# Sums of squares with tokens on partitions in the scan mixer of a two-block kernel

## The reference, cut to what matters

```python
kk = heads(k * k_k)                                   # [b, n, 12, 64]
kk = kk / jnp.maximum(jnp.sqrt(jnp.sum(kk * kk, axis=-1, keepdims=True)), 1e-12)
...
mu = jnp.mean(y, axis=-1, keepdims=True)              # y: sum of both directions' scans
var = jnp.mean(jnp.square(y - mu), axis=-1, keepdims=True)
yn = ((y - mu) * lax.rsqrt(var + GN_EPS)).reshape(b, n, D_RWKV) * gn_w + gn_b
```

## Time and profile before

| | us |
|---|---|
| runs, median of 3 (lowest to highest) | 3272.98 (3271.57 to 3274.49) |
| profiled execution, first to last instruction (span) | 3270.0 |
| TensorE matmuls busy | 3175.3 |
| VectorE busy | 2170.2 |
| ScalarE busy | 541.8 |
| GpSimd busy | 171.0 |

### The profile page before, as it was taken

One profiled execution on the slowest core, in us unless ns is written; L12 is line 12 of the kernel. 1 busy time (PEld: TensorE's weight loads), 2 busy tenths in 40 slices (PEclk: granted clock), 3 DMA queues, 4 the chain that ended last, 5 costly groups with the idle time before them and its releaser, 6 DMA issues.

```text
span 3270.0 us, 64614 instructions
## 1 busy us (share of the span) xinstructions
PE 3175.3 (97%) x28090; PEld 2861.1 (87%) x28090; DVE 2170.2 (66%) x4656; ACT 541.8 (17%) x1073; POOL 171.0 (5%) x200
## 2 busy tenths in 40 slices
PE   7999999899999999999999999999999999999998
PEld 3888445588888999999889999999999999999998
DVE  6887337566676476675657667776676576776774
ACT  2000010234433110110111011121110102120111
POOL 1000000122222010000000000000000000000000
PEclk9999999999999999999999999999999999999999
DMA  7456656100000245455245564334444443334443
GB/s 290 172 217 223 235 205 231 44 7 6 7 7 7 80 168 180 155 168 181 96 165 168 172 222 158 118 121 143 154 170 174 144 166 105 129 123 168 142 168 117
DMA packets 69229, 466.46 MB, mean 143 GB/s; under 512 B 7296, under 2 KB 9984, under 8 KB 16217
## 3 DMA queue, kind: packets, MB, share of 16 engines
q1 hardware_dynamic: 51696, 368.07, 32.2%
q0 software_dynamic: 12192, 87.04, 7.2%
q10 hardware_dynamic: 5065, 7.27, 0.7%
HBM read 456.59 MB, written 5.77 MB: 141 GB/s over the span
## 4 chain that ended last, share of the span: by engine, by line
PE 91%; DVE 6%; ACT 2%; DMA 1%; issue 1%; POOL 0%; ACTq 0%; DVEq 0%; POOLq 0%
PE ps L785 32%; PE ps L1279 18%; PE ps L840 8%; PE ps L680 7%; PE ps L1430 4%; PE ps L864 4%; PE ps L902 1%; PE ps L915 1%; PE ps L921 1%; PE ps L1298 1%; PE ps L1176 1%; PE ps L1353 1%; PE ps L1224 1%; PE ps L1328 1%; DMA arena<-in_ada_t 1%; PE ps L962 1%
## 5 line engine op out<-in xcount | busy, mean ns | idle before, releaser
L785 PE MATMUL ps<-arena 128*128 128x128 f32 x4400 | 519.1, 275 | 0.0
L785 PEld LDWEIGHTS ps<-arena 128*128 128x128 f32 x4400 | 505.0, 192 | 0.0
L785 PE MATMUL ps<-arena,ring 128*128 128x128 f32 x2200 | 275.0, 275 | 0.0
L1875 DVE TENSOR_TENSOR arena<-arena,ps 128x256 f32<-128x256 f32 x146 | 61.5, 421 | 309.4 <-ACT arena L1481 283.5
L785 PEld LDWEIGHTS ps<-arena,ring 128*128 128x128 f32 x2200 | 260.9, 192 | 0.5
L2005 DVE CUSTOM_DVE_ANT_0 arena<-arena,vec 128x1024 f32<-128x1024 f32 x168 | 206.7, 1281 | 1.7 <-DMA arena<-in_ada_t 1.6
L1279 PE MATMUL ps<-y,arena 128*128 128x128 f32 x1584 | 193.3, 276 | 0.6 <-DVE y L2502 0.6
L1279 PEld LDWEIGHTS ps<-y,arena 128*128 128x128 f32 x1584 | 184.6, 192 | 4.8 <-issue 3.4
L1840 DVE TENSOR_TENSOR arena<-ring 128x512 f32<-128x512 f32 (+1 forms) x170 | 113.9, 670 | 61.2 <-DMA ring<-in_w_f_down 33.3
L680 PE MATMUL ps<-arena,ring 128*128 128x512 f32 x352 | 152.2, 592 | 0.0
L680 PEld LDWEIGHTS ps<-arena,ring 128*128 128x128 f32 x352 | 66.9, 190 | 83.8 <-issue 83.7
(11 more groups left out here) (395 smaller groups left out, 5847.6 us busy)
## 6 DMA issues: line engine op xcount, KB each, us to landing
ring<-in_w_f_gu SPq DMA_DIRECT2D x88, 1024.0 KB, 4.9
arena<-in_ada_t POOLq DMA_DIRECT2D x72, 1024.0 KB, 5.3
ring<-in_w_fx_gu SPq DMA_DIRECT2D x44, 1024.0 KB, 4.8
ring<-in_w_f_down SPq DMA_DIRECT2D x36, 1024.0 KB, 4.8
ring<-in_w_fx_down SPq DMA_DIRECT2D x24, 1024.0 KB, 4.8
ring<-in_w_qk_a SPq DMA_DIRECT2D x18, 1024.0 KB, 4.8
ring<-in_w_qk_r SPq DMA_DIRECT2D x16, 1024.0 KB, 4.8
ring<-in_w_v_r SPq DMA_DIRECT2D x16, 1024.0 KB, 4.8
```

The costliest lines, as they stand in the source:

```text
L785: last = mm(out, weights[number][:, j * P:(j + 1) * P], inputs[number](base + j), start=(s.opens and j == 0 and number in (1, 5)), stop=(s ...
```

## The change

The squares become the stationary operand of a product whose moving operand is two columns of `blk`, the first column of each head. The result has tokens on partitions: for the keys four chunks of 128 tokens by two heads, 8 columns (`key_rows`), for the readout two chunks, 4 columns (`y_rows`). Clamp, root and reciprocal work on these. To bring the scales back to channels on partitions, one product for each chunk and head has the column, repeated 64 times, as stationary operand and the identity as moving operand (`key_back`, 8 products; `readout_back`, 4 products); VectorE then multiplies from PSUM (`key_unit` for the keys, in one piece of 512 columns). `key_back` is at step 5 of an even unit, behind `chunk_u`; `readout_back` at step 8. The readout's last four VectorE operations move to step 9. `key_products` waits for one more step. For t = 0, `key_back` is behind all slots of e_in, `key_inverse` ahead of slot 9 on VectorE, `key_unit` behind slot 10, and TensorE starts the mixer after it.

```diff
+        def head_columns():
+            return blk[:, 0:P:64]
+        def back_bank(u):
+            return 3 if unit(u) else 6
+        def over_head(rows, c, hd):
+            return rows[:, c, hd:hd + 1].to_broadcast([P, 64])
...
-                mm(ps[:, norm_sums(t), :], blk[:], kk, start=True, stop=True).then_inc(*step(f"pe.kk_sum{t}"))
+                for c in range(4):
+                    last = mm(ps[:, norm_sums(t), 2 * c:2 * c + 2], kk[:, c * P:(c + 1) * P], head_columns(), start=True, stop=True)
+                last.then_inc(*step(f"pe.kk_sum{t}"))
+
+            def key_back(t):
+                pe.wait_ge(*past(f"dve.kk_rows{t}"))
+                for c in range(4):
+                    for hd, rows in enumerate((FIRST, SECOND)):
+                        last = mm(ps[rows, norm_sums(t), c * P:(c + 1) * P], over_head(key_rows, c, hd), ident[:],
+                                  start=True, stop=True)
+                last.then_inc(*step(f"pe.kk_back{t}"))
...
+            key_back(0)
...
-            pe.wait_ge(*past("dve.kk_max0"))
+            pe.wait_ge(*past("dve.kk0"))
...
+                        pe.wait_ge(*past(f"dve.gn_n{t}"))
...
-                mm(ps[:, 5, 0:SEQ], blk[:], gn_sq, start=True, stop=True).then_inc(*step(f"pe.gn_var{t}"))
+                for c in range(LAT):
+                    last = mm(ps[:, 5, 2 * c:2 * c + 2], gn_sq[:, c * P:(c + 1) * P], head_columns(), start=True, stop=True)
+                last.then_inc(*step(f"pe.gn_var{t}"))
+
+            def readout_back(t, u):
+                pe.wait_ge(*past(f"dve.gn_rows{t}"))
+                if unit(u):
+                    pe.wait_ge(*past(f"act.k_tok{u}"))
+                for c in range(LAT):
+                    for hd, rows in enumerate((FIRST, SECOND)):
+                        last = mm(ps[rows, back_bank(u), c * P:(c + 1) * P], over_head(y_rows, c, hd), ident[:], start=True, stop=True)
+                last.then_inc(*step(f"pe.gn_back{t}"))
...
+                    elif n == 5 and u:
+                        key_back(u // 2)
...
+                if t is not None and n == 8:
+                    readout_back(t, u)
...
-                f(kk, kk, ACT.Sqrt).then_inc(*step(f"act.kk_std{t}"))
+                rows = key_rows.rearrange("p c h -> p (c h)")
+                f(rows, rows, ACT.Sqrt).then_inc(*step(f"act.kk_std{t}"))
...
-                ts(kk, ps[:, norm_sums(t), :], 1e-24, None, ALU.max).then_inc(*step(f"dve.kk_max{t}"))
-
-            def key_inverse(t, n):
+                ts(key_rows.rearrange("p c h -> p (c h)"), ps[:, norm_sums(t), 0:8], 1e-24, None, ALU.max) \
+                    .then_inc(*step(f"dve.kk_max{t}"))
+
+            def key_inverse(t):
                 v.wait_ge(*past(f"act.kk_std{t}"))
-                half = slice(SEQ * (n // 2 - 2), SEQ * (n // 2 - 1))
-                nc.vector.reciprocal(kk[:, half], kk[:, half]).then_inc(*step(f"dve.kk_inv{t}_{n}"))
-                v.wait_ge(*past(f"dve.kk_inv{t}_{n}"))
-                tt(kk[:, half], kk[:, half], kkr[:, half], ALU.mult).then_inc(*step(f"dve.kk{t}_{n}"))
+                rows = key_rows.rearrange("p c h -> p (c h)")
+                nc.vector.reciprocal(rows, rows).then_inc(*step(f"dve.kk_rows{t}"))
+
+            def key_unit(t):
+                v.wait_ge(*past(f"pe.kk_back{t}"))
+                tt(kk, ps[:, norm_sums(t), :], kkr, ALU.mult).then_inc(*step(f"dve.kk{t}"))
...
-                elif s.l == 9:
-                    key_inverse(0, 4)
-                    key_inverse(0, 6)
+                elif s.l == 10:
+                    key_unit(0)
...
-                    elif n in (4, 6) and u:
-                        key_inverse(u // 2, n)
+                    elif n == 4 and u:
+                        key_inverse(u // 2)
+                    elif n == 6 and u:
+                        key_unit(u // 2)
...
-                        nc.vector.reciprocal(gn_std, gn_std).then_inc(*step(f"dve.gn_rstd{t}"))
-                        v.wait_ge(*past(f"dve.gn_rstd{t}"))
-                        tt(gn_cen, gn_cen, gn_std, ALU.mult).then_inc(*step(f"dve.gn_n{t}"))
-                    elif n == 8:
+                        rows = y_rows.rearrange("p c h -> p (c h)")
+                        nc.vector.reciprocal(rows, rows).then_inc(*step(f"dve.gn_rows{t}"))
+                    elif n == 9:
+                        v.wait_ge(*past(f"pe.gn_back{t}"))
+                        tt(gn_cen, gn_cen, ps[:, back_bank(u), 0:SEQ], ALU.mult).then_inc(*step(f"dve.gn_n{t}"))
```

More of the change, by code:

```diff
@@ L382, in program @@
         mid, carry = take(2, 4), take(3, 4)
+        key_rows, y_rows = take(4, 2), take(2, 2)
         tri = y[:, 1, 0:4, :].rearrange("p (q x) t -> p q (x t)", q=2) \
@@ L1608, in fill @@
                         act.wait_ge(*past(f"pe.gn_var{t}"))
-                        f(gn_std, ps[:, 5, 0:SEQ], ACT.Sqrt, bias=V("gneps"), scale=1.0 / 64) \
+                        f(y_rows.rearrange("p c h -> p (c h)"), ps[:, 5, 0:2 * LAT], ACT.Sqrt, bias=V("gneps"), scale=1.0 / 64) \
                             .then_inc(*step(f"act.gn_std{t}"))
@@ L2130, in key_clamp @@
                 v.wait_ge(*past(f"pe.kk_sum{t}"))
-                ts(kk, ps[:, norm_sums(t), :], 1e-24, None, ALU.max).then_inc(*step(f"dve.kk_max{t}"))
-            def key_inverse(t, n):
+                ts(key_rows.rearrange("p c h -> p (c h)"), ps[:, norm_sums(t), 0:8], 1e-24, None, ALU.max) \
+                    .then_inc(*step(f"dve.kk_max{t}"))
+            def key_inverse(t):
                 v.wait_ge(*past(f"act.kk_std{t}"))
-                half = slice(SEQ * (n // 2 - 2), SEQ * (n // 2 - 1))
-                nc.vector.reciprocal(kk[:, half], kk[:, half]).then_inc(*step(f"dve.kk_inv{t}_{n}"))
-                v.wait_ge(*past(f"dve.kk_inv{t}_{n}"))
-                tt(kk[:, half], kk[:, half], kkr[:, half], ALU.mult).then_inc(*step(f"dve.kk{t}_{n}"))
+                rows = key_rows.rearrange("p c h -> p (c h)")
[3 more added lines that the diff above has]
+                tt(kk, ps[:, norm_sums(t), :], kkr, ALU.mult).then_inc(*step(f"dve.kk{t}"))
             for s in slots_flat("e_in"):
+                if s.l == 9:
+                    key_inverse(0)
                 v.wait_ge(slots_used, s.n + 1)
@@ L2315, in fill @@
                     elif n == 7:
-                        v.wait_ge(*past(f"dve.kk{u // 2}_6"))
+                        v.wait_ge(*past(f"dve.kk{u // 2}"))
                         key_scales(u)
```

## The result

The changed kernel takes 3285.54 us, the median of five runs (3284.59 to 3286.08), against 3272.93 (3271.51 to 3274.49) for the kernel before on the same chip: ratio 1.004, 95% interval 1.0029 to 1.0051, or 12.6 us more. 3286.0 was predicted.

The account below looks back on a forecast made before the run. The prediction took TensorE's in-order matmuls to bound the kernel. Its terms, 4.3 + 2.5 + 1.0 + 1.8 + 0.75 + 2.8 = 13.1 us, on 3273.0 gave 3286 us, range 3277 to 3294.

Parts of the forecast that it names:

- the start: Hand-over from e_in to the mixer: features waits for the last slot's whole handling and the unit key, +4.3 us.
- the readouts: Ordinary readouts: readout_back costs TensorE 0.75 us, up to 0.3 of it hidden; net +0.45, four times, +1.8 us.
- p = 12: Readout at p = 12: TensorE is never idle there, so readout_back's full 0.75 us counts.
- the end: Last readout: readout_back stands behind ten e_out products, with VectorE's four operations only after it, +2.8 us.
- the even units: Even units, t = 1 to 5: key_back fills the hole at level_x 4; +0.2 us a unit, +1.0 in all.
- the clock: After TensorE's 4.2 us gap before features: half-speed matmuls over features and Fourier products, +2.5 us (0 to +3.5).
- (a): Rival: the clock holds over the new gap before features, 3283.5 us; chance 0.16.
- the factor of 1.45: Step for key_back: gain from alternating, taken from L1053 against L1058, turning 0.108 us a record into 0.075.
- (b): Rival: column halves do not overlap at all in the return products, 0.108 us a record, 4.2 us more, 3290; chance 0.17.
- Around the span: Outside the profiled span: 3.0 us between the span of 3270.0 and the runs' median of 3272.98, taken to stay.
- (d): Rival: VectorE's relief spreads and all 21.9 us of TensorE's idle time in the steady part goes, 3269 us; chance 0.05.
- (e): Rival: the start gap is absorbed, say because ScalarE's part is the limit anyway, 3279 us; chance 0.08.

Follow-up runs that it names:

- Numbers 1: Changed kernel with key_back(0) before the products of e_in slot 10 and key_unit(0) after the copy of slot 9: 3279.1 us, ratio 1.0020 to the kernel before.
- number 3: Changed kernel with five unused 512-column products between key_back(0) and features, the wait for the key kept: 3283.7 us, ratio 1.0033 to the kernel before.
- number 8: The kernel of number 5 with key_back's two loops exchanged, one column half after the other: 3277.0 us, ratio 1.0013 to the kernel before.
- number 2: Changed kernel with the last readout's readout_back after five of the ten e_out products, five behind it: 3281.0 us, ratio 1.0025 to the kernel before.
- number 5: Changed kernel with only the keys by columns, first unit's hand-over mended, readouts as in the kernel before: 3274.5 us, ratio 1.0002 to the kernel before.
- number 10: Key units 1 to 5 by columns, earlier reciprocal, key_back and key_of; unit 0 and readouts as in the kernel before: 3268.9 us, ratio 0.9988 to it.

## Why the prediction was right

The sum was 13.1 us and 12.6 came. Four terms were right, the start, the readouts, p = 12 and the end: 9.65 us written, 9.7 by the distances. Two missed in opposite directions: the even units by 2.0 us, and the clock, to which the medians leave 3.8 us (12.6 less 8.8) where 2.5 was written. That these two nearly cancel is luck.

- **The start, 4.3.** 4.45 by the distance; 4.6 us of waiting where 4.2 was written. Right. Numbers 1 and 3 show the cause: the wait goes with the order and stays when only the gap is filled.
- **The clock, 2.5.** Right in kind and place: granted 0.51 over the 7 us from the gap's end on, 1.00 with the gap filled (number 3). The size there was 3.0 (3.5, less the 0.6 that the kernel before loses a little later). Filling the gap made the whole kernel only 1.8 us faster, so as a term of its time 3.0 may be too much; whether the rest comes back as other dips is not shown. Chance (a), the clock holds, failed. That idling halves the clock is what the Trainium skill says (TensorE: Matmul & The Clock Gate, The HAM clock gate), and numbers 1 and 3 agree: granted 1.00 where the gap is gone or filled.
- **The even units, +1.0.** The mechanism was right: level_x 4's wait gone, the hole filled by key_back. The size was off. key_back took 1.02 us, my lower bound, and not 1.35, so its records overlap at the 0.055 of the earlier trace rows and not at the 0.075 that the factor of 1.45 gave. And 0.17 of it lay under a wait that I had not counted: before, level_t 3 came 0.76 us after chunk_u's start, of which the products take 0.59 (913.23 to 913.82 here). The new sums saved 0.07 more (0.94 us against 1.01). So level_t 3 came only 0.78 later (16.17 us behind features, 15.39 before), the chain from there to level_x 4 became 0.97 shorter (2.43 us, not 3.40), and the unit gained 0.19 instead of losing 0.2. Five times, -0.95, where +1.0 was written. The step that was mis-sized is "So key_back costs 16 x 0.075 + 0.15 = 1.35 us", and with it "level_t 3 starts 907.1 instead of 905.92". Chance (b), no overlap, failed; number 8 shows what a poorer order costs. The rule of the Trainium skill that the prediction weighed (TensorEngine Tiling (Array Packing), Tiling Modes, Key Properties), that different tiles work in parallel, agrees with number 8. Of the drain at a change of mode the trace shows a cost, but not that it is a drain: the pairs of key_back start 0.109 us apart, but the second follows the first after 0.16 and the next shape follows the last pair after 0.21, together 0.15 more. That is the 0.15 of the sum, which no row ahead of the prediction shows by itself.
- **The readouts, +1.8.** 0.48, 0.48, 0.48 and 0.47, together 1.9. Right.
- **p = 12, +0.75**, measured 0.73. **The end, +2.8**, measured 2.64, of which number 2 returns 2.0 by order alone.
- **Around the span.** I put 3.0 us there, the span against the median. The changed kernel's run shows 1.8 (3286.08 against 3284.3). All runs on record have 1.7 to 1.9, so the profiled execution of before was a quick one, and the 3.0 held 1.2 us of run-to-run spread. As the sum was of differences, it did no harm.
- **The rivals.** (d), VectorE's relief spreads: in the steady part only 3.8 us of waits went. It was out as predicted, for the reason given: the other two waits follow operations that the change does not touch. (e), the start is absorbed: no. VectorE lost 32.9 us of work, 34 predicted, and what TensorE had waited for in it was only what filled the five holes at level_x 4.

## What to carry to other kernels

Relief of an engine off the critical path is worth only the holes that end in it, and what the bound engine does in exchange is paid in full beyond them: here, over 385 us, 26 us off VectorE took 3.8 us off TensorE's waits, and the new work on TensorE used them up and 0.9 us more (the keys gave back 0.19 us five times, the readouts took 0.47 four times). The worst costs were at the ends of the loop, where a new dependency met an engine with no other unit to work on; look there first, and shift the order (five products on each side of the new ones) before giving up the idea. And a fast step pays only when the order around it is made anew: the same key edit went from no measurable change (number 5) to 3.6 us faster (number 10) by moving key_back and key_of one step forward, the reciprocal two, and leaving unit 0 alone.

## What the runs showed of the hardware

- Products of two columns are not cheap: eight records took 0.94 us (905.21 to 906.15), as much as one product of 512 columns in two records (1.01, 897.07 to 898.08).
- Sixteen records of 128 x 64 stationary took 1.02 us with the column halves alternating and 1.51 with each half in turn. Alternating, they start in pairs 0.007 us apart, a pair every 0.109 us; in turn, four of each half start beside each other around the switch.
- A TensorE wait of 4.6 us was followed by 7 us at a granted clock of 0.51, some 3 us lost; five useless products in the gap kept the clock and made the kernel 1.8 us faster. The dips of about 3.4 us that the clock takes anyway are worth 1.7 us each where TensorE is the bound (2154.4, 2156.1 and 2157.7 us from the norm after the mixer to the end, with one, two and three of them), and the spread of 8 us between runs of one kernel goes with the mean granted clock of the run (0.996 to 0.994).
- VectorE's reciprocal of eight columns took 0.20 us and of four 0.18, against 1.75 for 256.
